# The gate input of the per-layer stage put and fetched by ACT's queue instead of SyncE's

## The reference

```python
y = _rms(h, norm_ffn_g[i])
h = h + (jax.nn.silu(y @ w_gate[i]) * (y @ w_up[i])) @ w_down[i]
y = _rms(h, norm_ple_g[i])
h = h + jax.nn.sigmoid(y @ w_ple_gate[i]) * (p[i] @ w_ple_proj[i])
```

## Time and profile before

| what | value |
|---|---|
| median of 3 runs | 1392.72 us (1392.12 to 1393.17) |
| the profiled execution | 1394.26 us, of which the span of its instructions 1392.5 us |
| PE busy | 1384.1 us, 99% of the span |
| DVE, ACT, POOL busy | 1112.8, 817.6 and 105.4 us |
| PE's granted clock | 1.00 in every stretch (2.4 GHz, the higher level) |
| DMA | 338.25 MB, mean 243 GB/s |

### The profile page before, as it was taken

One profiled execution on the slowest core, in us unless ns is written; L12 is line 12 of the kernel. 1 busy time (PEld: TensorE's weight loads), 2 busy tenths in 40 slices (PEclk: granted clock), 3 DMA queues, 4 the chain that ended last, 5 costly groups with the idle time before them and its releaser, 6 DMA issues.

```text
span 1392.5 us, 16787 instructions
## 1 busy us (share of the span) xinstructions
PE 1384.1 (99%) x6239; PEld 1134.0 (81%) x6239; DVE 1112.8 (80%) x1325; ACT 817.6 (59%) x1104; POOL 105.4 (8%) x94
## 2 busy tenths in 40 slices
PE   9999999999999999999999999999999999999998
PEld 7888888888888888888888888888778887777887
DVE  6589976766898987889898878877577669896796
ACT  7476755555666545666655566655466556665453
POOL 2000010000000000000000000000000144330000
PEclk9999999999999999999999999999999999999999
DMA  9766656887989748888985779896778688899654
GB/s 332 248 207 212 204 172 201 274 274 207 284 262 267 202 170 265 265 275 234 268 254 183 257 237 267 242 320 226 271 243 294 204 266 260 253 271 295 196 205 151
DMA packets 178250, 338.25 MB, mean 243 GB/s; under 512 B 12561, under 2 KB 36365, under 8 KB 178040
## 3 DMA queue, kind: packets, MB, share of 16 engines
q1 hardware_dynamic: 158968, 289.56, 63.8%
q0 software_dynamic: 6112, 22.44, 7.3%
q10 hardware_dynamic: 13088, 25.18, 6.0%
HBM read 295.14 MB, written 26.26 MB: 231 GB/s over the span
## 4 chain that ended last, share of the span: by engine, by line
PE 94%; DVE 3%; DMA 2%; ACT 0%; issue 0%; SPq 0%; POOL 0%; POOLq 0%; ACTq 0%; DVEq 0%
PE acc L2013 15%; PE acc L2015 14%; PE acc L2014 14%; PE acc L2202 13%; PE acc L2199 13%; PE acc L2201 13%; DVE w_lo L1275 1%; PE sp L2199 1%; PE sp L2202 1%; PE sp L2201 1%; PE tp L2202 1%; PE tp L2201 1%; PE tp L2199 1%; PE acc L2075 1%; DMA parked<-tile 1%; PE sp L2304 1%
## 5 line engine op out<-in xcount | busy, mean ns | idle before, releaser
L858 ACT ACTIVATE w_hi<-w_raw 128x1024 fp32r<-128x1024 f32 x481 | 502.4, 1057 | 378.3 <-PE acc L2015 225.3
L1275 DVE TENSOR_TENSOR w_lo<-w_raw,w_hi 128x1024 fp32r<-128x1024 f32 x470 | 570.0, 1227 | 181.8 <-ACT w_hi L858 176.7
L2013 PE MATMUL acc<-w_lo,hh 128*128 128x512 f32 x528 | 208.1, 394 | 0.0
L2015 PE MATMUL acc<-w_hi,hl 128*128 128x512 f32 x528 | 205.9, 390 | 0.0
L2014 PE MATMUL acc<-w_hi,hh 128*128 128x512 f32 x528 | 205.8, 390 | 0.0
L2199 PE MATMUL acc<-w_lo,yh 128*128 128x512 f32 x460 | 179.2, 389 | 0.0
L2201 PE MATMUL acc<-w_hi,yh 128*128 128x512 f32 x460 | 179.1, 389 | 0.0
L2202 PE MATMUL acc<-w_hi,yl 128*128 128x512 f32 x460 | 179.1, 389 | 0.0
L2013 PE MATMUL acc<-w_lo,yh 128*128 128x512 f32 x416 | 162.7, 391 | 2.4 <-DVE w_lo L1275 2.4
L2015 PE MATMUL acc<-w_hi,yl 128*128 128x512 f32 x416 | 162.1, 390 | 0.0
L2014 PE MATMUL acc<-w_hi,yh 128*128 128x512 f32 x416 | 162.0, 390 | 0.0
(11 more groups left out here) (283 smaller groups left out, 1938.5 us busy)
## 6 DMA issues: line engine op xcount, KB each, us to landing
w_raw<-in_w_gate SPq DMA_DIRECT2D x88, 512.0 KB, 5.6
w_raw<-in_w_up SPq DMA_DIRECT2D x88, 512.0 KB, 5.4
w_raw<-in_w_down SPq DMA_DIRECT2D x88, 512.0 KB, 5.8
w_raw<-in_w_in SPq DMA_DIRECT2D x64, 512.0 KB, 4.5
w_raw<-in_swa_w_in ACTq DMA_DIRECT2D x48, 512.0 KB, 5.4
w_raw<-in_w_out SPq DMA_DIRECT2D x32, 512.0 KB, 4.8
w_raw<-in_w_ple_gate SPq DMA_DIRECT2D x32, 512.0 KB, 6.3
w_raw<-in_swa_w_out SPq DMA_DIRECT2D x32, 512.0 KB, 5.8
```

What stands on the lines that cost most here:

```text
L858: act.activation(w_hi[:, v % SPL], src, ACT.Copy).then_inc(hi_ready, 1)
L1275: dve.tensor_tensor(w_lo[:, v % SPL], src, w_hi[:, v % SPL].bitcast(F32), ALU.subtract).then_inc(lo_ready, 1)
L2013: pe.matmul(dst, xh[:, f, tk], w_lo[:, v % SPL, k], start=(f == 0), stop=False)
L2015: last = pe.matmul(dst, xl[:, f, tk], w_hi[:, v % SPL, k], start=False, stop=(f == CK * n - 1))
```

## The change

ACT's queue, not SP's, issues the puts and fetches of the four groups. Groups 1 and 3 get a DRAM scratch of their own, `parked_odd`, with a semaphore of its own, `odd_out`. Each fetch stands two or three chunks behind its put in ACT's list, and the high part three chunks behind the fetch:

| group | put after | fetch after | high and low part after (before: ) |
|---|---|---|---|
| 0 | T15 | T18 | T21 (T19) |
| 1 | T17 | T20 | T23 (T22) |
| 2 | P0 | P2 | P5 (P3) |
| 3 | P6 | P8 | P11 (P9) |

DVE's addition of the fourth group of columns moves from after P3 to after P4, its turn from after P4 to after P5 (behind the low part of group 2), ACT's square from after P4 to after P5, and DVE's request for the norm from after P5 to after P6.

```diff
+        def scratch_of(n):
+            return parked_odd if n in (T_PLE + 1, T_PLE + 3) else parked
+
+        def out_of(n):
+            odd = (T_PLE + 1, T_PLE + 3)
+            return (odd_out, 1 + odd.index(n)) if n in odd else (blocks_out, n + 1 - sum(n > o for o in odd))
...
@@ SyncE: @@
-                if n == 22:
-                    move(T_PLE)
             for n, (j, c) in enumerate(DOWN):
                 load(START[PLE_UNIT] + n, wpg_v, CK * c, CW * j)
-                if n == 0:
-                    move(T_PLE + 1, freed=T_PLE - 1)
-                if n == 6:
-                    move(T_PLE + 2, freed=T_PLE)
-                if n == 12:
-                    move(T_PLE + 3, freed=T_PLE + 1)
...
@@ ScalarE: @@
+            def put_ple(j):
+                n = T_PLE + j
+                if j >= 2:
+                    act.wait_ge(turned, 64 * (n - 1))
+                act.wait_ge(blocks_done, n + 1)
+                act.dma_start(scratch_of(n)[:, :], turn_buffers(n)[0]).then_inc(out_of(n)[0], 16)
+
+            def fetch_ple(j):
+                n = T_PLE + j
+                act.wait_ge(turned, 64 * n)
+                act.wait_ge(turned_lo, low_count(T_PLE - 1 if j < 2 else n - 2))
+                landed, count = out_of(n)
+                act.wait_ge(landed, 16 * count)
+                blocks = scratch_of(n).rearrange("(q j) (r m) -> r j q m", q=4, r=4)
+                for r in range(4):
+                    part = turn_buffers(n)[1][32 * r:32 * (r + 1)].rearrange("p (q m) -> p q m", q=4)
+                    act.dma_start(part, blocks[r]).then_inc(turned, 16)
...
-                if n in (19, 22):
-                    ple_turned_high((19, 22).index(n))
+                if n in (15, 17):
+                    put_ple((15, 17).index(n))
+                if n in (18, 20):
+                    fetch_ple((18, 20).index(n))
+                if n in (21, 23):
+                    ple_turned_high((21, 23).index(n))
...
                 split(START[PLE_UNIT] + n)
-                if n == 3:
+                if n == 0:
+                    put_ple(2)
+                if n == 2:
+                    fetch_ple(2)
+                if n == 5:
                     ple_turned_high(2)
-                if n == 4:
                     wait_left(act, PLE_UNIT - 1)
                     square(2, 3)
-                if n == 9:
+                if n == 6:
+                    put_ple(3)
+                if n == 8:
+                    fetch_ple(3)
+                if n == 11:
                     ple_turned_high(3)
...
@@ VectorE: @@
                 split(START[PLE_UNIT] + n)
-                if n == 3:
+                if n == 4:
+                    add_resid(PLE_UNIT - 1, 3)
+                if n == 5:
                     ple_turned_low(2)
-                    add_resid(PLE_UNIT - 1, 3)
-                if n == 4:
                     wait_left(dve, PLE_UNIT - 1)
                     turn(T_PLE + 3, resid[:, :, 3 * CW:])
-                if n == 5:
+                if n == 6:
                     request(R_PLE, 24)
-                if n == 9:
+                if n == 11:
                     ple_turned_low(3)
```

More of the change, by code:

```diff
@@ L284, in build @@
     parked = nc.dram_tensor("parked", (P, 1024), F32, kind="Internal").ap()
+    parked_odd = nc.dram_tensor("parked_odd", (P, 1024), F32, kind="Internal").ap()
     parked_w = [nc.dram_tensor(f"parked_w{i}", (P, 1024), F32, kind="Internal").ap() for i in range(NG)]
@@ L426, in build @@
         blocks_out = sem("blocks_out")
+        odd_out = sem("odd_out")
         turned_hi = sem("turned_hi")
@@ L593, in put @@
                 sp_.wait_ge(blocks_done, n + 1)
-                sp_.dma_start(parked[:, :], turn_buffers(n)[0]).then_inc(blocks_out, 16)
+                sp_.dma_start(scratch_of(n)[:, :], turn_buffers(n)[0]).then_inc(out_of(n)[0], 16)
             def from_quarters(dst, scratch, landed):
@@ L602, in fetch @@
             def fetch(n):
-                sp_.wait_ge(blocks_out, 16 * (n + 1))
-                from_quarters(turn_buffers(n)[1], parked, turned)
+                landed, count = out_of(n)
+                sp_.wait_ge(landed, 16 * count)
+                from_quarters(turn_buffers(n)[1], scratch_of(n), turned)
             def put_mixed(i):
@@ L1781, in _ @@
                     turn(T_PLE + d, resid[:, :, CW * d:CW * (d + 1)])
-                if n in (19, 22):
-                    ple_turned_low((19, 22).index(n))
+                if n in (21, 23):
+                    ple_turned_low((21, 23).index(n))
             def add_gated(j):
```

## The result

| | before | changed |
|---|---|---|
| median | 1392.33 us (1391.87 to 1395.71, 11 runs) | 1398.15 us (1394.23 to 1399.20, 11 runs) |
| ratio to before, 95% interval | | 1.0030 (1.0022 to 1.0039) |
| span of the profiled execution | 1392.5 us | 1396.6 us |
| mean granted clock of PE in the runs | 1.000 in the profiled one | 1.000 in the three runs near 1394.3 us, 0.997 to 0.999 in the eight from 1397.4 us up |

Forecast were 1389.8 us with a range of 1389.1 to 1392.1 us, and a chance of 0.06 for a time more than 0.2% longer. The measured time is longer and outside the range. The medians stand 5.8 us apart (0.42%); the ratio over all runs is smaller, since three of the changed kernel's eleven lie near 1394.3 us and two of before's above 1395.5.

A forecast was written before the change was run, and what follows sets the result against it. PE bounds the kernel, busy 1384.1 of 1392.5 us; its gate-input stalls cost 3.01 us. Removing them and adding 0.05 us for group 2 takes the median 1392.72 to 1389.8 us, range 1389.1 to 1392.1 us.

The forecast's parts named there:

- the part on group 2: At P4: fetch landing 5.6 to 7.6 us after issue, group 2 ready within 0.05 us of its time; cost 0.05 us.
- that gives nothing: SP's queue: it loads weights earlier, but no wait for weights is among this stretch's waits, so no gain.
- group 0: Its fetch on ACT's queue lands 5.6 to 7.6 us after first issue; T21's split up to 1.2 us late, cost 0.
- The put: Group 2's put on ACT's queue, nothing of its own ahead: 4.3 to 5.9 us, against 9.58 us on SP's queue.
- Rival A: Group 2's put no faster on ACT's queue, P4 1.3 to 3.4 us late; 1392.0 us, chance 0.13.
- Rival B: ACT's in-order list blocks on landings, no chunk is split, 5.9 us of new stalls; 1395.6 us, chance 0.06.
- The gain: PE's two stalls between P0 and P12, at P4 and P10, cost 3.01 us, all removed by the change.
- The issues: ACT's four DMA issues per fetch run beside a split: cost 0, without that cover at most 0.7 us each.
- Group 3: Its fetch lands by 1007.3 to 1010.9, P12's split is ready in time; cost 0, with 1.9 us to spare.
- the order of ACT and DVE: Same instructions on DVE and ACT in another order around the gate input's chunks: cost 0.

The follow-up runs named there:

- hold_four: Changed kernel, but SP's loads of P2, P4, P9 and P17 each wait for a group's fetch to land; 1392.73 us, ratio to before 0.9997.
- hold_two: Changed kernel, but only SP's load of P9 waits, until group 2's fetch has landed; 1393.45 us, ratio to before 1.0001.
- sp_queue: Changed kernel's order on ACT and DVE, but SP's queue issues the puts and fetches, each fetch behind further loads; 1392.28 us, ratio to before 0.9997.
- late_parts: Kernel before, SP unchanged, with groups 2 and 3's high and low parts placed later; 1391.67 us, ratio to before 0.9991.
- order_only: Changed kernel's places on ACT and DVE, but SP puts and fetches as in the kernel before, with one scratch; 1392.30 us, ratio to before 0.9998.
- before_again: The kernel before, unchanged, run once more for a second trace; 1391.67 us, span 1389.9 us.
- fill: Changed kernel with 12 unused 128x128 matmuls ahead of PE's wait at P4; 1395.87 us, ratio to before 1.0021.
- hold_zero: Changed kernel, but only SP's load of P2 waits, until group 0's fetch has landed; 1397.28 us, ratio to before 1.0036.
- traffic: hold_two plus four unused 512 KB copies within DRAM on POOL's queue during group 2's fetch; 1398.62 us, ratio to before 1.0050.
- after_again: The changed kernel, unchanged, run once more for a second trace; 1398.09 us.

## Why the prediction was wrong

1. **The step that failed** is in the part on group 2: "Landed 5.6 to 7.6 us later". Both durations were read from fetches of SP's queue, ahead of which SP had stood still from the put on. The change removes that standstill, and the prediction said of it only that SP "loads earlier" and "that gives nothing". The rows were right; the condition under which they held went with the change. The same fetch took 11.3 and 11.8 us. The same error sits in group 0 (9.1 us, up to 7.6 forecast) and group 3 (12.1 us); group 1's was quick, 4.1 us for its longest DMA with 0.73 MB beside it.
2. **The put** was forecast at 4.3 to 5.9 us and took 4.4. That it passes SP's loads on a queue of its own was right, and Rival A, which had the put slow, fell: its sign, PE waiting for `yl` at P4, came, but by the fetch. In the other traces of ACT's queue this put took 4.5 to 5.5 us, and 7.2 us in hold_four, so it is not free of its neighbours either. The Trainium skill, "DMA: Bandwidth & Descriptors", section "Queues, rings and completion order", says that each DMA engine serves the rings in turn; the 4.4 us in place of 9.58 agree. The same rule read from the other side says that loads on SP's ring pass a fetch on ACT's, and the same page's section "Issuing engines are not separate DMA queues" that DMAs of all issuing engines run on the same 16 DMA engines and interleave; 2.40 MB beside 0.52 MB in 11.2 us agree with that. Rival A set the right rule against the wrong transfer.
3. **Rival B** named the mechanism that did occur, ACT's list held by a landing: T21's split came 3.0 us late. The splits kept their lead over PE, and what it cost was the late put of group 2. hold_two, issued just as late, had no pause, so by itself that was harmless. B's sum had P4 start at 1000.1 us, and it started at 1000.46; that is luck, for B had a put of 10.1 and a fetch of 7.6 us, and they took 4.4 and 11.3.
4. **The clock** had no term. In the earlier trace rows it is full throughout and the pauses there are 1.2 and 2.0 us from start to start. The pause of 4.0 us was followed by 12 matmuls at half the clock: 2.56 us, two thirds of the pause's own price.
5. **The gain** was mis-sized too. The 3.01 us came from one execution, which lay 1.9 us above the median of 11 runs, and were subtracted from the median. The second trace lost 0.4 us there. Three executions were traced that lose nothing in the stretch: they took 1391.8 (sp_queue), 1392.0 (late_parts) and 1392.9 us (order_only), and the medians of these kernels lie 0.6, 1.0 and 0.4 us below before's, none of them clear of no change. So at most about 1 us was there to win, and the forecast 1389.8 us lies below every run of every kernel here (the lowest took 1391.05).
6. **The issues** were put at nothing, or 0.7 us at most. That holds where they ran beside a split (961.68). Where the queue had waited for a landing they held ACT for their whole 1.9 us: T21's split behind 970.83, and P3's at 987.02, 1.0 us late. PE noticed neither.
7. **Group 3** was given 1.9 us to spare. In the changed kernel its fetch took 12.1 us (1006.1 to 1018.2, at the latest 1010.9 forecast), and P12 did not wait only because PE was 6.4 us late itself: luck. In hold_two, where PE was on time at P4, P12 started 0.45 us late.
8. **Right:** the order of ACT and DVE costs nothing that the runs can tell (order_only).

## What to carry to other kernels

A queue that stands still between two dependent transfers keeps the DMA engines free for the second one. Before that standstill is taken away, the duration of the second must be read from a place where loads run beside it, or the loads must be held for its time; one wait did it here. Where the expected gain is as small as the distance between the profiled execution and the median, a second trace says first whether there is a gain at all. And a place further down in the list for the consumer, with no change of queues, can take the same waits away (late_parts), if there is a wait to take.

## What the runs showed of the hardware

- Four DMAs of 128 KB from DRAM, in rows of 1 KB: group 2's longest took 2.8 us with 0.2 MB moved beside them (before_again, order_only), 4.1 to 4.7 us beside 0.5 to 0.7 MB (hold_four, hold_two, before), 7.4 us beside 1.6 MB (sp_queue), and 8.9 to 10.6 us beside 2.1 to 2.8 MB (fill, hold_zero, changed kernel twice, traffic), no matter whether that came from SP's or POOL's queue. The amounts are those of the fetch's own time. In the changed kernel the fetch's 0.52 MB were moved in the time in which SP's queue moved 2.40.
- A put of 512 KB took 4.4 to 7.2 us on ACT's queue (seven traces of group 2), and 6.7 to 9.6 us on SP's queue right behind six loads (order_only, late_parts, before_again, before).
- A pause of PE of 4.0 us between two matmuls' starts was followed by 12 matmuls at half the granted clock, 5.3 us long, one of 4.2 us (after_again) by 13, and one of 2.9 us in hold_zero (996.54 to 999.40) by eight, from the third on (granted clock 0.52 from 1000.0 to 1003.4 us). Pauses of 1.2 and 2.0 us (before) were followed by none, and in fill, where matmuls filled the pause, the clock stayed at 1.00.
